# A mixture-of-experts layer on one core: a tenth weight block is fetched into the residual's memory, and the residual is turned back later

## The reference

```python
def expert_choice_ffn(h, w_router, w_gate, w_up, w_down):
    b, t, d = h.shape
    cap = EC_CAPACITY * t // N_EXPERTS                      # 2 * 512 / 16 = 64
    aff = jax.nn.softmax(jnp.einsum('btd,de->bte', h, w_router).astype(jnp.float32), axis=-1)
    gate, idx = lax.top_k(jnp.swapaxes(aff, 1, 2), cap)
    xs = jax.vmap(lambda hb, ib: hb[ib])(h, idx)
    hid = jax.nn.silu(jnp.einsum('becd,edf->becf', xs, w_gate)) * jnp.einsum('becd,edf->becf', xs, w_up)
    ys = jnp.einsum('becf,efd->becd', hid, w_down) * gate[..., None].astype(h.dtype)
    return jax.vmap(lambda ib, yb: jnp.zeros((t, d), yb.dtype).at[ib.reshape(-1)].add(yb.reshape(-1, d)))(idx, ys)
...
        x = x + g1 * mx
        hx2 = modulate(rms_norm(x, norm_ffn[l]), sh2, sc2)
        x = x + g2 * expert_choice_ffn(hx2, w_router[l], w_gate[l], w_up[l], w_down[l])
```

## Time and profile before

| | |
|---|---|
| time, median of 3 runs | 2161.07 us (2160.69 to 2161.09) |
| span of the profiled execution | 2159.6 us |
| TensorE matmuls busy | 2011.6 us (93%) |
| VectorE busy | 921.3 us (43%) |
| ScalarE busy | 568.8 us (26%) |
| moved from and to HBM | 529.05 MB, mean 245 GB/s |
| 16 DMA engines between 600 and 1300 us | busy throughout, 427 to 428 GB/s |
| stretch of the expert weights | from 325 to about 1337 us |

### The profile page before, as it was taken

The page is one execution under the profiler, slowest core; times in us unless marked ns, Lnnn a source line. Parts: engine busy times, 40 slices in busy tenths (PEclk is TensorE's granted clock), DMA queues, the critical chain, the costliest instruction groups (busy, mean ns, idle before and its releaser), DMA issues.

```text
span 2159.6 us, 23580 instructions
## 1 busy us (share of the span) xinstructions
PE 2011.6 (93%) x9832; PEld 1255.7 (58%) x9832; DVE 921.3 (43%) x1484; ACT 568.8 (26%) x879; POOL 60.5 (3%) x107
## 2 busy tenths in 40 slices
PE   7999999899889899898989988998999999999998
PEld 5888777443333334242424324775588888888886
DVE  4665674320101111111101003777787656666555
ACT  5433313100000000000000002337535444334445
POOL 1000010000000000000000000004300000000000
PEclk9999999899999999999999999999999999999999
DMA  9462116699999999999999997141123232323231
GB/s 341 161 229 79 40 60 252 254 387 418 428 428 427 429 428 427 428 428 428 427 427 428 427 428 306 61 117 40 40 84 112 88 117 78 117 78 108 79 115 50
DMA packets 107802, 529.05 MB, mean 245 GB/s; under 512 B 15037, under 2 KB 43825, under 8 KB 82865
## 3 DMA queue, kind: packets, MB, share of 16 engines
q1 hardware_dynamic: 107697, 527.55, 61.2%
HBM read 525.43 MB, written 2.10 MB: 244 GB/s over the span
## 4 chain that ended last, share of the span: by engine, by line
PE 84%; DMA 6%; DVE 5%; issue 3%; ACT 2%; POOL 1%; SPq 0%; POOLq 0%; ACTq 0%; DVEq 0%
PE bank L999 22%; PE bank L602 14%; PE bank L603 14%; PE bank L604 14%; PE bank L1050 6%; DMA f<-in_w_gate_dram 5%; PE bank L960 3%; PE bank L973 3%; PE bank L613 2%; DMA f<-in_w_in_dram 1%; PE bank L1247 1%; PE bank L1138 1%; ACT high L1692 1%; PE bank L807 1%; DVE high L2302 1%
## 5 line engine op out<-in xcount | busy, mean ns | idle before, releaser
L999 PE MATMUL bank<-f,high 128*64 128x512 f32 x2048 | 469.3, 604 | 48.6 <-issue 31.6
L602 PE MATMUL bank<-r 128*128 128x512 f32 (+1 forms) x1016 | 403.4, 397 | 13.7 <-DVE high L2125 4.7
L603 PE MATMUL bank<-r 128*128 128x512 f32 (+1 forms) x1016 | 398.8, 393 | 0.0
L604 PE MATMUL bank<-r 128*128 128x512 f32 (+1 forms) x1016 | 398.3, 392 | 0.0
L999 PEld LDWEIGHTS bank<-f,high 128*64 128x64 f32 x2048 | 153.0, 138 | 335.1 <-issue 320.3
L2277 DVE SCALAR_TENSOR_TENSOR f<-bank,low,f 128x512 f32<-128x512 f32 x64 | 48.0, 750 | 505.7 <-PE bank L973 505.7
L1050 PE MATMUL bank<-f,high 128*64 128x512 f32 x1024 | 230.4, 608 | 18.8 <-issue 18.8
L1400 ACT ACTIVATE high<-bank 128x512 f32<-128x512 f32 (+2 forms) x93 | 51.4, 583 | 677.7 <-PE bank L613 335.8
L602 PEld LDWEIGHTS bank<-r 128*128 128x128 f32 (+1 forms) x1016 | 191.0, 188 | 65.8 <-issue 9.8
L603 PEld LDWEIGHTS bank<-r 128*128 128x128 f32 (+1 forms) x1016 | 191.2, 188 | 42.1 <-issue 1.7
L604 PEld LDWEIGHTS bank<-r 128*128 128x128 f32 (+1 forms) x1016 | 190.8, 188 | 41.8
(11 more groups left out here) (360 smaller groups left out, 1734.4 us busy)
## 6 DMA issues: line engine op xcount, KB each, us to landing
f<-in_w_up_dram SPq DMA_DIRECT2D x64, 2048.0 KB, 21.7
f<-in_w_down_dram SPq DMA_DIRECT2D x64, 2048.0 KB, 21.4
f<-in_w_gate_dram SPq DMA_DIRECT2D x63, 2048.0 KB, 21.5
f<-in_w_in_dram SPq DMA_DIRECT2D x13, 2048.0 KB, 7.9
f<-in_w_up_dram SPq DMA_DIRECT2D x22, 1024.0 KB, 6.9
high<-in_w_ada_dram SPq DMA_DIRECT2D x32, 512.0 KB, 5.3
f<-in_w_ada_dram SPq DMA_DIRECT2D x4, 2048.0 KB, 15.3
f<-in_w_out_dram SPq DMA_DIRECT2D x4, 2048.0 KB, 7.8
```

Of the source, the lines that this page charges most:

```text
L602: pe.matmul(o, wh, xh, start=first, stop=False)
L603: pe.matmul(o, wl, xh, start=False, stop=False)
L604: return pe.matmul(o, wh, xl, start=False, stop=last)
L999: ins = pe.matmul(o[64 * e:64 * e + 64, :], xsT[p % 2][:, 2 * k + r, 64 * e:64 * e + 64], ws[e](2048 * r + 512 * fc), start=k == 0 and r = ...
```

## The change

- Block 9, the second block of the first up products, no longer takes a slot of the ring. It is fetched into XT's own memory as soon as the last half row of token rows has been turned. The other blocks keep the seven slots; the table that gives slots exchanges two pairs of slots on the way, so that the last blocks lie where the next stage allows it.
- XT is overwritten by that, so H2 now holds unscaled token rows with their columns in order (a plain copy), and after the first pair's up products a new function `turn_again` turns H2 back in 8 groups of 4 transposes on TensorE, with 8 copies to XT on ScalarE. VectorE's first `combine` waits for those.
- The norm `rtok` moves from the copy of H2 into the selection matrix: instead of one compare of 128 x 512 there are eight `tensor_scalar` of 128 x 64 (compare, then multiply by the token's factor). The affinities are multiplied by the root once, to make up for it in `gate_mask`.
- `gather` reads every second column of H2, since the columns are no longer regrouped.

```diff
@@ the tables of slots
-        NTH = {n: i for i, n in enumerate(n for n in range(NBLK) if n not in (2, 7))}
-        RING = {i: n for n, i in NTH.items()}
+        once_w = own(4096, XT_AT)
+        slot_order = list(range(NSLOT))
+        SLOT_OF, FILLED, BEFORE, held = {}, {}, {}, {}
+        for m, n in enumerate(n for n in range(NBLK) if n not in (2, 7, 9)):
+            if m == 18:
+                slot_order[4], slot_order[5] = slot_order[5], slot_order[4]
+            if m == 24:
+                slot_order[3], slot_order[4] = slot_order[4], slot_order[3]
+            i = SLOT_OF[n] = slot_order[m % NSLOT]
+            BEFORE[n] = held.get(i)
+            FILLED[n] = FILLED.get(held.get(i), 0) + 1
+            held[i] = n
@@ SyncE
-                m = NTH[n]
-                i = m % NSLOT
-                if m >= NSLOT:
-                    used = moe_used(RING[m - NSLOT])
+                if n == 9:
+                    sp.wait_ge(s["pe_route"], val("pe_route", "h2", 3, 1))
+                    sp.dma_start(once_w, src).then_inc(s["mw"], 16)
+                    continue
+                i = SLOT_OF[n]
+                if BEFORE[n] is not None:
+                    used = moe_used(BEFORE[n])
@@ TensorE
-                    ins = pe.matmul(o, H2[:, t, 128 * k:128 * k + 128], Sp[i][:, t, :], start=t == 0, stop=t == 3)
+                    ins = pe.matmul(o, H2[:, t, 256 * (k // 2) + k % 2:256 * (k // 2) + 256:2], Sp[i][:, t, :],
+                                    start=t == 0, stop=t == 3)
...
+            def turn_again(j):
+
+                o = take(("again", j), "xt_again", j)
+                up(turn_blocks(o, [H2[:, t, 128 * j:128 * j + 128] for t in range(4)]), "pe_again", j)
...
+                if p == 0:
+                    for j in range(8):
+                        turn_again(j)
                 if p < 7:
                     gates(p + 1)
                 turn_h(p, 0)
@@ ScalarE
-                    up(a.activation(o, bank("h2", t, half).rearrange("p (k c r) -> p k r c", k=2, r=2), ACT.Copy,
-                                    scale=rtok[:, t:t + 1]), "a_route", "h2", t, half)
+                    up(copy(H2[:, t, 512 * half:512 * half + 512], bank("h2", t, half)[:, :]), "a_route", "h2", t, half)
...
+                if p == 0:
+                    for j in range(8):
+                        a.wait_ge(s["pe_again"], val("pe_again", j))
+                        up(copy(XT[:, j, :], bank("again", j)[:, :]), "xt_again", j)
                 for fc in range(4):
                     a.wait_ge(s["pe_up"], val("pe_up", "h", p, fc))
@@ VectorE
-                up(v.tensor_tensor(s4, io, sl, ALU.is_equal), "v_gather", "sp", p)
+                for t in range(4):
+                    for e in range(2):
+                        ins = v.tensor_scalar(Sp[i][:, t, 64 * e:64 * e + 64], iota1, slotT[:, t, 2 * p + e:2 * p + e + 1],
+                                              rtok[:, t:t + 1], ALU.is_equal, ALU.mult)
+                up(ins, "v_gather", "sp", p)
...
+                    if p == 0:
+                        v.wait_ge(s["xt_again"], val("xt_again", d))
...
             gather(0, range(8))
+            up(v.tensor_tensor(aff, aff, roott.unsqueeze(2).to_broadcast([P, 4, 16]), ALU.mult), "v_route", "affr")
+            own_wait("v_route")
             gate_mask(0)
```

More of the change, by code:

```diff
@@ L20 @@
 DMA_SEMS = (*(f"g{i}" for i in range(6)), *(f"cg{i}" for i in range(4)), *(f"zf{i}" for i in range(4)), "x0", "x1", "rows0", "rows", "small", "ctx", "ada0", "ada1", "ada2", "ada3", "w0", "w1", "ptok", "out",
-            *(f"m{i}" for i in range(7)), "mx", "my", "mg0", "mg1", "mh0", "mh1", "mq0", "mq1")
+            *(f"m{i}" for i in range(7)), "mx", "my", "mw", "mg0", "mg1", "mh0", "mh1", "mq0", "mq1")
 SEMS = (
@@ L27 @@
     "a_proj", "v_proj", "a_gla", "v_gla", "state", "a_fill", "v_fill", "g_y",
-    "a_mix", "v_mix", "xt", "sq", "sqs", "wsq", "a_route", "v_route", "v_gather", "a_up", "v_up", "hT", "ys",
+    "a_mix", "v_mix", "xt", "sq", "sqs", "wsq", "a_route", "v_route", "pe_again", "xt_again", "v_gather", "a_up", "v_up", "hT", "ys",
     "a_fin1", "v_fin1", "v_norm", "u2h", "u2l_v", "a_z", "v_z", "taps", "a_cmp", "v_cmp", "a_att", "v_att", "g_att",
@@ L195, in build_program @@
         gain12, rtok, brow = small[:, 560:568], small[:, 568:572], small[:, 576:592]
+        roott = small[:, 595:599]
         q2 = v3(mem(2048, M + 8192), 4)
@@ L514, in sync @@
                             src = I["w_down"][0, 14 + e_][512 * k:512 * k + 512, :].rearrange("(p r) n -> p (r n)", p=P)
-                            sp.dma_start(moe_slot[NTH[n - 1 + e_] % NSLOT][:, c0:c1], src[:, c0:c1]).then_inc(s[f"{name}{e_}"], 16)
+                            sp.dma_start(moe_slot[SLOT_OF[n - 1 + e_]][:, c0:c1], src[:, c0:c1]).then_inc(s[f"{name}{e_}"], 16)
             for c in range(N1, NC_):
@@ L982, in landed_block @@
                     return lambda c: once_y[:, c:c + 512] if c < 3072 else once_z[:, c - 3072:c - 2560]
-                i, filled = NTH[n] % NSLOT, NTH[n] // NSLOT
-                pe.wait_ge(s[f"m{i}"], 16 * (filled + 1))
+                if n == 9:
+                    pe.wait_ge(s["mw"], 16)
+                    return lambda c: once_w[:, c:c + 512]
+                i = SLOT_OF[n]
+                pe.wait_ge(s[f"m{i}"], 16 * FILLED[n])
                 return lambda c: moe_slot[i][:, c:c + 512]
@@ L1607, in scalar @@
             a.wait_ge(s["pe_route"], val("pe_route", "aff"))
-            up(a.activation(rtok, v3(bank("aff")[:, 0:256], 4)[:, :, 32], ACT.Sqrt, bias=epst), "a_route", "root")
+            up(a.activation(roott, v3(bank("aff")[:, 0:256], 4)[:, :, 32], ACT.Sqrt, bias=epst), "a_route", "root")
             a.activation(small[:, 593:594], epst, ACT.Exp)
@@ L1614, in scalar @@
                     a.wait_ge(s["pe_route"], val("pe_route", "h2", t, half))
-                    o = H2[:, t, 512 * half:512 * half + 512].rearrange("p (k r c) -> p k r c", k=2, r=2)
-                    up(a.activation(o, bank("h2", t, half).rearrange("p (k c r) -> p k r c", k=2, r=2), ACT.Copy,
-                                    scale=rtok[:, t:t + 1]), "a_route", "h2", t, half)
+                    up(copy(H2[:, t, 512 * half:512 * half + 512], bank("h2", t, half)[:, :]), "a_route", "h2", t, half)
             for p in range(8):
@@ L2203, in vector @@
             v.wait_ge(s["a_route"], val("a_route", "root"))
-            up(v.reciprocal(rtok, rtok), "v_route", "rtok")
+            up(v.reciprocal(rtok, roott), "v_route", "rtok")
             own_wait("v_route")
@@ L2241, in gather_masks @@
                 i = p % 2
[L2242 to L2245, removed]
                 if p > 1:
```

## The result

| | before | after |
|---|---|---|
| median | 2159.42 us (10 runs) | 2165.04 us (10 runs) |
| ratio, 95% interval | | 1.0027, 1.0019 to 1.0035 |
| span of the profiled execution | 2159.6 us | 2167.0 us |

The change makes the kernel 5.8 us slower (0.0027 x 2159.4), with an interval of 4.1 to 7.6 us. With the later runs the median of before lies 1.65 us lower than where the prediction started from.

A forecast was written before the change was run, and what follows sets the result against it. The prediction took TensorE's pace up to block 23's release, then the full weight stream, as the bound; 0 + 3.86 + 1.1 = +5.0 us there gave 2166.0 us against 2161.07, range 2163.0 to 2168.5.

The forecast's parts named there:

- What bounds the kernel: Start of the experts: TensorE's pace sets the first pair up to 493 us; block 23's release then sets the end.
- Part 1: Weight stream: block 9 fetched early into XT leaves block 23's release the same event; gain 0.
- Part 2: After the last up step: 32 transposes delay block 23's release by 3.86 us; ScalarE's copies cost nothing.
- Part 3: VectorE's mask before the first gather: eight small pieces cost 1.1 us more, ends 0 and 1.2.
- Rival A: Cheap pieces: mask costs only 0 to 0.4 us more, transposes run without a hitch; 2165.1 us, chance 0.18.
- Part 4: Gathers reading every second column, and the rest: 0 us; upper end 1.5 us for 128 records before block 23's release.
- one of the signs that I had named: In the gathers: the forecast would be wrong if they take longer than before.
- The sum: At block 23's release and the end: 0 + 3.86 + 1.1 = +5.0 us, giving 2166.0 against 2161.07 us.
- Rival B: Weight stream is the limit after all: 4.9 us come back, transposes hide in TensorE's slack; 2157.3 us, chance 0.09.
- Rival C: First step of the experts: longer mask wait keeps TensorE's clock low, adding 3.4 us; 2169.4 us, chance 0.09.
- The hole before block 23: Weight stream: DMA engines would stand still about 7 us before block 23; forecast wrong if that hole is gone.
- The first gather and block 23: Start of the experts: first gather near 408.4 us, issue of block 23 near 498; forecast wrong if before 496.

The follow-up runs named there:

- e2: Changed kernel with block 9 back in the ring by the earlier slot table, turning back kept; 1.0031 of the kernel before.
- e10: Changed kernel, own slot table, with turning back behind the third and fourth down steps and the mask told of in pieces; 1.0001 of the kernel before.
- e7: Changed kernel with block 17 also fetched into XT after block 9, slot exchanges redone, turning back behind the third and fourth down steps; 0.9994 of before.
- e8: As e7, but VectorE tells TensorE of the mask after each two of its eight pieces; 0.9993 of the kernel before.
- e1: Changed kernel without the turning back (no 32 transposes, no eight copies, residual lost); 2161.1 us, 1.0009 of the kernel before.
- e3: Changed kernel with two groups of four transposes moved behind each of the four down steps of pair 0; 1.0015 of the kernel before.
- e4: Changed kernel with one 128 x 512 compare per mask and gathers reading neighbouring columns, result not the reference's; 1.0013 of the kernel before.

## Why the prediction was right

**What bounds the kernel.** Right. B to C is 823.0 to 823.9 us in the nine profiles with seven places, while B itself lies anywhere between 492.75 and 501.11. The end of the experts hangs on the release of block 23.

**Part 1, block 9: 0.** Right (e2, e10). Only the place was wrong at which the stream waits the gain away: not before block 23, but around 460 (e2). The reason given, that the ring's distance from block 17 on is still seven, is confirmed from the other side by e7 and e8, where a real eighth place moved the last hole and gave 3.1 us.

**Part 2, turning back: 3.86 us.** The mechanism was right, the size 0.36 too large: 3.50 us (e1, e3). The row that I took it from has a pause of 0.24 us in TensorE's weight loads, behind the first eight (from 339.49 to 339.73 in the kernel before), and here TensorE ran through: 36 loads in one row of 3.91 us, 36 transposes in 4.15 us. What the pause waited for the trace doesn't show, nor where the other 0.12 us come from. ScalarE's copies took 4.03 us and hid, as forecast.

**Part 3, the mask: 1.1 us.** It was 1.19 us. The working gave 1.89 us for the eight pieces and the trace has 1.88; I had then moved toward a row of one operand, needlessly. The advice of the Trainium skill on small tiles ("VectorE: DVE Perf Modes", the section on the TRN2 errata) held in direction, and the estimate from its fixed term, 1.5 us, was too low for operations with two per-partition operands. Rival A (cheap pieces) is out.

**Part 4, strided reads: 0.** This term failed, and with it one of the signs that I had named: the gathers do take longer than before. The earlier trace rows compared single loads of 64 columns, one of 16 partitions and one of 128, which says little of what a run of gathers takes. At the full clock 16 records went from 2.05 to 2.15 us, 5%, and 0.69 us in all, nearly half of the upper end given (1.5). That bound took 0.11 us for a record at full clock; it is 2.05 / 16 = 0.128. The 0.69 is inferred from the rows of e4 and of the changed kernel, which differ in the mask besides, but the mask isn't in those records.

**The sum.** 5.0 us forecast; 3.50 + 1.19 + 0.69 = 5.4 us by the traces, and 5.8 us by the timed runs, their interval holding both. (Against the first profile of before it is 5.5, as its first 16 gather records took 3.65 us where all others but e10's took 3.73 to 3.76.) In part that is luck: 0.36 us too much in part 2 stand against 0.09 too little in part 3 and 0.69 in part 4. So is the distance to the measured 2165.04, since 2161.07 was 1.65 us too high to start from. **Rival A** had 2165.1, nearer still. The times can't tell it from my forecast; only the mask's 1.88 us in the trace, 1.19 more than before where A had 0 to 0.4, do. **Rival B** (the stream) fell with e1 and e2. **Rival C** (the clock) has its place but not its cause: the first step did take 7.52 to 8.05 us in the changed kernels with the whole mask, but also 8.01 in e4 and 8.30 in the kernel before, and 7.09 in all three with the mask in pieces. What decides it is open; on the timed runs it can't have weighed more than the 0.4 us between 5.4 and 5.8 and what their interval leaves.

**The signs that I named.** The hole before block 23 was to be about 7 us. It was 5.4 by the four stretches from 496 to 504, and I had the wrong reason for it: I put it down to the missing block, which was waited for around 460, and it came from the later release. e2 has 5.1 us there without any early block. The first gather and block 23 came where I had put them (408.4 and 498) once the 0.95 us from ahead of the mask, and for block 23 the 0.73 us of the first step, are taken off: 408.5 and 498.6. The rest of the kernel kept its length: from C to the end of the span it is 843.2 us in both.

## What to carry to other kernels

A block fetched early into spare memory helps only if it lengthens the distance at which the last hole in the stream is released; count that distance behind the last hole, not where the memory is idle. In a stage that ends at the pace of a stream, work placed just ahead of the release that refills it cost its full time here (3.5 us), and the same work behind that release cost nothing measurable (e3). Where slots of a ring are exchanged, check each pair against the steps that free its slots.

## What the runs showed of the hardware

- Reading every second float32 column as the stationary operand made a run of 128 x 128 products 5% slower at the full clock (16 records in 2.15 instead of 2.05 us) and no slower at the clock of 0.50 (3.75 us in both forms). I had expected nothing. The Trainium skill, "SBUF — State Buffer", section on the DMA port swizzle, says that float32 accesses that hit a line of 16 bytes at least twice keep the full bandwidth, which would make this stride free; the measurement decides, and it is nearly but not quite free.
- A `tensor_scalar` of 64 float32 with two per-partition operands takes 310 ns and the next one starts 0.22 us later (eight in 1.88 us); I had worked out 311 ns and 0.226 us from rows of 256 and 512 elements.
- The same 32 records of the first gate step took 7.09 to 8.30 us, also between two profiles of one program, since the granted clock rises from 0.50 to 1.00 at a moment that isn't the same in each. In the two profiles of the kernel before, TensorE works without a pause from the first gather on (407.32 and 406.52); the mean granted clock is 0.64 from 410 to 411 and 1.00 behind it in the one, and 0.66 from 412 to 413 and 1.00 behind it in the other. The waits for the mask ahead of it were 1.16 and 1.15 us, so they don't decide it.
- The last step of the routing, which no kernel here changes, started between 405.25 and 410.25 us in thirteen profiles. The two of the kernel before are among the early ones (406.27 and 405.47). Whether that is chance wasn't settled. In the changed kernel's profile 0.87 of its 0.95 us are there at 354, ahead of every edited instruction, and A to B and B to C leave it out.
